# A two-layer chunked-attention and latent-attention trunk on eight cores: row factors spread by DMA, a gate projection that is scaled after its product, and a ready-first instruction order

## What is computed

```python
def rmsnorm(x, g):
    xf = x.astype(jnp.float32)
    y = xf * lax.rsqrt(jnp.mean(xf * xf, axis=-1, keepdims=True) + EPS)
    return (y * g.astype(jnp.float32)).astype(x.dtype)

h = x                                        # (16, 2048, 1024) f32
for i in range(2):
    xn = rmsnorm(h, norm_mix[i])
    z = xn @ w_in[i]                         # 1024 -> 3008
    q_a, k_a, v_a, gate_a, c_q, c_kv, k_rope_raw, gate_b = split_cols(z, IN_SIZES)
    o_a = chunked_relpos_attention(...)      # 8 heads of 64, chunks of 64, band of 576 keys, learned bias
    o_b = mla_attention(...)                 # 4 heads, rmsnorm(c_q), rmsnorm(c_kv), rotary part, chunk-causal
    mixed = jnp.concatenate([o_a * jax.nn.silu(gate_a), o_b * jax.nn.silu(gate_b)], axis=-1)
    h = h + mixed @ w_out[i]
    gate = jax.nn.sigmoid(rmsnorm(h, norm_ple[i]) @ w_pg[i] + b_pg[i])
    h = h + (p[i] @ w_pe[i]) * gate
return rmsnorm(h, norm_final)
```

## Time and profile before

| | |
|---|---|
| median of 3 runs | 2576.07 us (2574.05 to 2578.4) |
| the profiled execution, its time | 2576.03 us |
| its span, first to last instruction, core 7 | 2574.4 us |
| spans of the 8 cores | 2561.0 to 2574.4 us |
| phase 1, layer 0 | up to about 950 us |
| phase 2, layer 0 | to about 1298 us |
| phase 1, layer 1 | to about 2172 us |
| phase 2, layer 1 | to the end |

### The profile page before, as it was taken

The page is one execution under the profiler, slowest core; times in us unless marked ns, Lnnn a source line. Parts: engine busy times, 40 slices in busy tenths (PEclk is TensorE's granted clock), DMA queues, the critical chain, the costliest instruction groups (busy, mean ns, idle before and its releaser), DMA issues.

```text
span 2574.4 us, 45914 instructions; the slowest of 8 cores (2561.0 to 2574.4 us)
## 1 busy us (share of the span) xinstructions
PE 2186.2 (85%) x14928; PEld 1114.7 (43%) x14928; DVE 1263.1 (49%) x2623; ACT 1214.1 (47%) x2220; POOL 185.2 (7%) x509
## 2 busy tenths in 40 slices
PE   3788989898898788888869988989889878788786
PEld 2344545454454443444324444545445444344342
DVE  3466353535644425555556556253664442555655
ACT  2355555663655553434324455565355555233232
POOL 3000000000000110000020000000000000000000
PEclk9799999999999998999889999999999999888787
DMA  9522111121200693444130101011110043233521
GB/s 180 160 64 77 47 54 58 36 61 53 67 9 16 111 215 115 131 127 133 56 111 25 58 27 46 28 36 35 47 34 9 14 91 113 87 101 90 167 71 66
DMA packets 99326, 194.92 MB, mean 76 GB/s; under 512 B 11800, under 2 KB 28696, under 8 KB 96280
## 3 DMA queue, kind: packets, MB, share of 16 engines
q1 hardware_dynamic: 90168, 164.19, 20.0%
q0 software_dynamic: 8928, 27.79, 6.8%
HBM read 165.19 MB, written 54.53 MB: 85 GB/s over the span
## 4 chain that ended last, share of the span: by engine, by line
PE 67%; DVE 14%; issue 7%; ACT 6%; DMA 3%; SPq 1%; POOL 1%; DVEq 0%; ACTq 0%; POOLq 0%
PE psa L304 63%; DVE sb_sc L335 4%; ACT sb_pt L316 3%; PE psa L308 2%; DMA sb_xs<-x 2%; DVE sb_pt L322 2%; PE psa L312 2%; SPq L349 1%; DVE sb_sc L322 1%; DVE sb_qb L322 1%; DVE sb_mx L335 1%; DVE sb_pt L335 1%; POOL sb_rcs L322 1%; ACT sb_rb L316 1%; ACT sb_sq L316 1%
## 5 line engine op out<-in xcount | busy, mean ns | idle before, releaser
L316 ACT ACTIVATE sb_pt<-psa 128x512 bf16<-128x512 f32 x1248 | 660.7, 547 | 270.2 <-PE psa L304 251.3
L304 PE MATMUL psa<-sb_hb,sb_w 128*128 128x512 bf16 x2560 | 646.9, 383 | 26.9 <-DVE sb_wabs L339 18.5
L304 PE MATMUL psa<-sb_qb,sb_ckt 128*128 128x512 bf16 (+3 forms) x1280 | 347.3, 355 | 10.4 <-ACT sb_pt L316 8.9
L304 PEld LDWEIGHTS psa<-sb_hb,sb_w 128*128 128x128 bf16 x2560 | 233.3, 98 | 271.0 <-issue 75.0
L304 PE MATMUL psa<-sb_va,sb_pt 128*128 128x65 bf16 x2240 | 172.5, 198 | 92.6 <-DVE sb_pt L322 70.8
L304 PE MATMUL psa<-sb_qa,sb_ka 128*128 128x256 bf16 (+3 forms) x896 | 226.0, 309 | 18.6 <-ACT sb_pt L316 18.0
L304 PE MATMUL psa<-sb_ckvt,sb_pt 128*128 128x129 bf16 x2176 | 237.5, 222 | 4.3 <-DVE sb_onb L322 1.2
L304 PEld LDWEIGHTS psa<-sb_ckvt,sb_pt 128*128 128x128 bf16 x2176 | 171.4, 98 | 138.2 <-issue 30.8
L304 PEld LDWEIGHTS psa<-sb_va,sb_pt 128*128 128x128 bf16 x2240 | 124.5, 100 | 240.1 <-issue 223.5
L322 DVE TENSOR_TENSOR sb_pt<-sb_pt,sb_eb 128x256 bf16<-128x256 bf16 (+2 forms) x608 | 172.7, 294 | 102.7 <-ACT sb_pt L316 98.6
L335 DVE SCALAR_TENSOR_TENSOR sb_pt<-sb_pt,psa 128x512 f32<-128x512 f32 x128 | 88.1, 688 | 233.0 <-PE psa L304 185.2
(11 more groups left out here) (131 smaller groups left out, 2502.6 us busy)
## 6 DMA issues: line engine op xcount, KB each, us to landing
sb_xs<-x SPq DMA_DIRECT2D x116, 256.0 KB, 3.5
mixd<-sb_mx SPq DMA_DIRECT2D x128, 128.0 KB, 1.8
sb_xs<-h SPq DMA_DIRECT2D x56, 256.0 KB, 3.5
sb_w<-w_in POOLq DMA_DIRECT2D x24, 512.0 KB, 26.2
sb_cs<-ropes SPq DMA_DIRECT2D x16, 512.0 KB, 3.3
sb_sc<-mixd SPq DMA_DIRECT2D x8, 1024.0 KB, 6.7
sb_qb<-mixd SPq DMA_DIRECT2D x8, 1024.0 KB, 6.4
sb_hb<-w_out POOLq DMA_DIRECT2D x8, 512.0 KB, 6.9
```

The costliest lines, as they stand in the source:

```text
L304: S.op("pe", lambda h: h.matmul(out, lhsT=lhsT, rhs=rhs, start=start, stop=stop, skip_group_check=skip), reads=reads, writes=writes, inc=l ...
L316: S.op("act", lambda h: h.activation(out=out, in_=in_, func=func, **kw), reads=reads, writes=writes, cost=c)
```

## The change

1. `bcast` is gone. `row_out` writes the 128x4 factors to a row of 512 f32 in DRAM (512 elements of 4 bytes at separate addresses), `row_in` reads that row back into all 128 partitions. Both are issued by SP, and `row_in` waits there for `row_out` to land.
2. In `OP` ACT now makes `hb2` from the sum of each chunk (h times `norm_ple`, no row factor) at once, in one of two buffers; in `PLE` the row factor is applied after the product: DVE multiplies the PSUM bank by the row (`rbp`) before tanh. `PLE` now shares four banks (0 to 3) with `OP`, and the product with `w_pe` alternates between banks 4 and 5.
3. `Sched` is a list scheduler. It first fixes a legal order and its dependences, then takes for every engine the ready operation of lowest rank (all streams 0, T 1, P 2); operations of one stream may overtake each other where nothing forbids it. `LAT` is 0.12 us and the costs are changed; a DMA with a key that begins with `d_r` is costed at 2.2 us.
4. The rope table is stored once (3 stores for each group); two loads with repeating addresses spread it. The bias table of `prep_e` comes in two halves through the third gate buffer of `sb_sg`, not through `sb_ckt`.
5. `x_load` of group 0 no longer waits for the end of `PLE` of group 7; it uses three staging buffers.

```diff
@@ Sched
-    LAT = 0.25
+    LAT = 0.12
...
+    def arrange(self, ops, rank):
+        free = {e: 0.0 for e in self.ENGS}
+        pend = {e: [] for e in self.ENGS}
+        avail = {e: [] for e in self.ENGS}
...
+            pick = min(avail[e])
...
+            end = t + o.cost
+            free[e] = end
+            if o.key is not None:
+                if o.key.startswith("d_r"):
+                    end += 2.2
...
@@ row factors
-        def bcast(cols, cols_r, n, bk):
-            for j in range(n):
-                mm4(PS[bk][:, j * 128:(j + 1) * 128], bc_col(cols[:, j:j + 1], 128), ident_f[:],
-                    [cols_r, const_r], [PR[bk]], j == n - 1)
+        def row_out(cols, cols_r, key):
+            i = rowi[0]
+            rowi[0] += 1
+            dma(bass.AP(rows_d.tensor, rows_d[i, 0:1].offset, [[1, 128], [128, 4]]), cols, [cols_r], [rows_r[i]], key,
+                allow_slow_non_contiguous=True)
+            return i
+
+        def row_in(i, out, out_r, key):
+            dma(out, bass.AP(rows_d.tensor, rows_d[i, 0:1].offset, [[0, 128], [1, SL]]), [rows_r[i]], [out_r], key)
@@ S1
+            row_in(row_out(rcs[:, k, 0:4], rcs_r[k], "d_ro0"), scf(7), sc_r[7], "d_ri7")
+            row_in(row_out(rcs[:, k, 4:8], rcs_r[k], "d_ro1"), RB[:, 1, :], rb_r[1], "d_ri1")
             gate(T_GB + 1, 1 + b, 1)
-            bk = PB.next()
-            bcast(rcs[:, k, 0:4], rcs_r[k], 4, bk)
-            ACT(scf(7), PS[bk], AF.Copy, [PR[bk]], [sc_r[7]])
...
@@ OP
-                bk = PB.next()
+                bk = (PB if n == 0 else R4).next()
...
-                ACT(SQ[:, fc % 4, :], hch(b, fc), AF.Square, hall(b, fc), [sq_r[fc % 4]])
+                ACT(hb2(b, fc), hch(b, fc), AF.Copy, hall(b, fc) + [par_r], [hb2_r[b][fc]], scale=gple[:, l, fc:fc + 1])
+                square(l, n, "g", fc, SQ1, sq_r, hch(b, fc), hall(b, fc))
...
@@ PLE
-            bcast(rcs[:, k, 0:4], rcs_r[k], 4, 5)
-            ACT(RB[:, 0, :], PS[5], AF.Copy, [PR[5]], [rb_r[0]])
-            for c in range(8):
-                STT(hb2(c), hch(b, c), gple[:, l, c:c + 1], RB[:, 0, :], ALU.mult, ALU.mult, hall(b, c) + [par_r, rb_r[0]],
-                    [hb2_r[c]])
...
-                ACT(utf(ui), PS[by], AF.Tanh, [PR[by], par_r], pt_r[ui * 2:ui * 2 + 2], bias=hbpg[:, l, fc:fc + 1], scale=0.5)
...
+                TT(t_, PS[by], rbp(b), ALU.mult, [PR[by]] + rbp_r[b], tr_)
+                ACT(t_, t_, AF.Tanh, tr_ + [par_r], tr_, bias=hbpg[:, l, fc:fc + 1], scale=0.5)
+                if fc >= 1:
+                    fin(fc - 1)
...
@@ merge
-        S.merge(["T", "Q", "P", "X", "L", "R", "W", "V", "Z", "E"])
+        S.merge(["T", "P", "G", "F", "X", "L", "R", "W", "V", "Z", "E"],
+                {"T": 1, "P": 2})
```

439 lines of the change are left out of this document (239 added, 200 removed).

## The result

The changed kernel takes 3454 us (3442 to 3464 in three executions), the kernel before 2576 us (2574 to 2578): a ratio of 1.341, 95% interval 1.334 to 1.348. I had forecast 2359 us, with 2290 to 2450 as the range. It is 878 us slower, where I saw 217 us of gain.

What follows compares the result with a forecast made beforehand. PE's work was taken to bound phase 1, the row factor's path the phase 2 rounds. From 2576.0 us, −70 − 49 − 82 + 20 − 10 − 15 − 14 + 3 = −217 gave 2359 us, range 2290 to 2450.

Steps and rivals of the forecast that it cites:

- 49 and 82: Phase 2 rounds: gains in us for layer 0 (rounds 42.4 to 36.3) and layer 1 (47.7 to 37.5).
- I take 2.4 out (a little over the store, since its pieces are 4 bytes): Row factor's path in phase 2 rounds: the store lands in 2.4 us, with the load's 3.5 a pair takes 5.9.
- slow transfers: Rival, rounds and phase 1: a transfer pair takes 10 us instead of 5.9, giving 2445 us; chance 0.10.
- f32 products, −70: Phase 1: 192 f32 products of 0.363 us each leave PE, all of it counted as gain, −70 us.
- phase 1 is not bound by PE's work: Rival: half the 70 us becomes waits for ACT and DVE, row waits cost 35 instead of 20; 2409 us, chance 0.12.
- Rows in phase 1: Phase 1: DVE waits for the row transfers with attention's bias products behind it, +20 us (0 to 60).
- Order, −10: Phase 1: the ready-first list can fill PE's holes, mostly waits for bias products on DVE; −10 us.
- order fills the holes: Rival, phase 1: next group's work fills PE's short holes, 60 us fewer than the −10 term; 2300 us, chance 0.20.
- the order's model is too optimistic: Rival, phase 1: PE stands before each of 1248 attention units, 0.21 us each, 262 us in all; 2621 us, chance 0.05.
- The clock: Rival, phase 2 rounds: the denser stream is granted 0.86, 85 us more in 16 rounds; 2444 us, chance 0.05.
- Start, −15: Start: 40 fewer rope stores free DMA time, partly lost to weights going out earlier; −15 us (−30 to +5).
- Layer 1's final scaling: Phase 2 rounds of layer 1: final scaling adds 6.8 us, most fits into DVE's waits, 1.2 added, giving 37.5.

Runs made afterwards that it cites:

- products back: The changed kernel with its 72 row spreads done by f32 products and an ACT copy again: 2461.3 us, ratio 0.957 to the kernel before.
- quick pair: The changed kernel with a small f32 product and DVE copy before each row store, which then has 4 pieces of 512 bytes: 2567 us, ratio 0.998.
- the split: The kernel with products back, each spread by 8 bf16 products of high and low parts for 4 f32 ones: 2419.9 us, ratio 0.941.
- the list with the measured landings: The changed kernel with only its list's model changed, 20.6 us for the store and 5.4 for the load instead of 2.2 each: 3076.2 us.
- one wire: The split products with the positions' load ahead of x, and all transfers sharing 170 bytes a nanosecond in the list's model: 2421 to 2423 us.

## Why the prediction was wrong, point by point

- **Where the time is lost.** The change did act at the border from OP to PLE, as I had argued. With the products back phase 2 took 267 us and the rest 303 us, 52 and 96 less than before; my terms were 49 and 82.
- **The failed step: "I take 2.4 out (a little over the store, since its pieces are 4 bytes)".** It was 20.6. The step took the landing to go by the bytes moved and gave next to nothing for 512 neighbouring pieces of 4 bytes; the runs show that their crowding is the price, since the same 512 pieces land in 2.5 us when they lie 64 bytes apart, and with 4 whole pieces the pair takes about 5 us, near my 5.9. The bounds were wrong as well, 3.6 to 10.8 for a pair that takes 26: the nearest rows were large transfers, and none of them crowds its pieces. With the measured pair my own formula holds roughly: 4.6 + 20.6 + 5.7 + 0.85 − 7.8 = 24 us open, 32.7 + 24 = 57 us a round in layer 0 (502 / 8 = 63 measured), and in layer 1 once more some 23 us for the final scaling's row and its 6.8 us: 87 (692 / 8 = 86).
- **Beyond the failed step.** With the quick pair the kernel takes 2567 us, still 208 above my 2359. By the table some 65 us of that are in phase 1, 47 at the start and 68 in the rest; the four bullets on f32 products, rows, start and final scaling below say where. So the crowded store makes 887 us of the miss of 1095 (3454 − 2567), and the other 208 by themselves would have put the time outside my range.
- **What a page said.** The Trainium skill, "DMA: Bandwidth & Descriptors", Anatomy of one DMA, has about 2.0 us fixed, for transfers issued by POOL. The stores here are issued by SP; those without crowding land in 1.7 and 2.5 us, about that figure. Its Specifications have a read-modify-write under 512 bytes: pieces of 4 bytes land in 2.5 us if they are 64 bytes apart, so size alone costs little here. Whether such a read-modify-write is what crowded pieces pay for, no run shows.
- **The rival "slow transfers"** named the mechanism and priced it at 10 us a pair. Its argument against, that stores land in 1.8, was the same wrong row.
- **f32 products, −70:** too large by the half-clock share, 48 × 1.13 = 54 us of PE's work. That PE's work is the bound of phase 1 held: the split took away 24 × 0.52 = 12.5 us a layer, and 17 and 12 us came back as time, so the rival "phase 1 is not bound by PE's work" falls for this much of it.
- **Rows in phase 1:** +20 taken. With quick transfers (4 pieces of 512 bytes) phase 1 takes 1693 us in both layers, with products 1687; without their 54 us and with some 10 us of small products it would be 1643, so by this estimate the waits for rows cost 50 us even then (I had 48 before I took off what hides it). The slow store adds 161 + 159 = 320 us. Of these the list with the measured landings gets 191 back.
- **Order, −10:** −11 and +10 us in the two layers. Neither "order fills the holes" nor "the order's model is too optimistic" shows, so long as the model's landings are right. The kernel with products back is the test of this.
- **The clock** fell, but as a consequence: with 34 us waits it is 0.74, in the kernel with split products 0.97 over the whole span. The rival's lower level under a dense stream does occur, though not in the kept trace of the changed kernel: 0.82 on four cores for 150 us with one wire, at a price of 22 us.
- **Border of the layers, −14:** about −11. In 45 us around the last product with `w_pe` PE is idle 17.9 us before and 6.5 with products back, where S1 of layer 1 starts 0.5 us after that product.
- **Start, −15:** +31. That weights went first was named and taken too lightly: all 12 weight transfers go out within the first 10 us, where ten of them went out from 21.5 us on before, and land in 41 us (20 before); the second group's x comes behind them. That this is the whole 31 us is not shown.
- **Layer 1's final scaling:** 1.2 us taken for a round. With quick transfers it is 48.5 − 34.6 = 14 us over layer 0. Part of it is that DVE's list and SP's queue have it ahead of the next group's row: PE's wait there is 6 us longer in the mean.
- **What I had said would refute it** did: landings of 2.4 us, a hole of 3 to 4 us, a clock above 0.95. It was 20.6, 34 and 0.74. One sign was reckoned wrong: with no hole the two transfers would take under 2.3 us together (5.9 − 3.6), not each.

## What to carry to other kernels

Before a scatter of small pieces is put on a path, look where the pieces fall in memory. Turning them into whole stretches first was measured as a working kernel; spreading them 64 bytes apart made the store quick, but a load that collects them again was not run. And if no transfer in the trace has that shape, its price has no upper bound from the trace and belongs in the range. A reduction or spread that PE does in 0.6 us is hard to beat by two transfers, since a pair costs about 5 us in the median even when quick and up to 11.9 in traffic, and can block the lists of SP and of the engine that waits. A model that orders a list should be fed with landings from a trace of the same traffic; with 20.6 and 5.4 in place of 2.2 us the same kernel was 378 us faster.

## What the runs showed of the hardware that I had not expected

- Stores of the same 2 KB landed in 2.5 to 20.6 us, by how close their separate pieces lie. 128 pieces of 4 bytes: 10.8 us side by side, 1.7 us 64 bytes apart.
- The crowded store and the load behind it took 26.3 to 26.7 us in the median on every core, though the store alone was seen at 13.5 on one and at 20.6 on another.
- A load of 512 pieces of 512 bytes took 4.7 us from four stretches, 11.5 us when all read the same 512 bytes.
- Four cores of one kernel were granted 0.82 for 150 us in which PE was busy nearly all the time, while the other four had 1.00 in the same stretch of the same program.
